# Modulation products in plain fp32 from the unsplit chunk on four column groups, and a latent projection in chunks of 352 columns

## The reference

```python
silu_c = jax.nn.silu(c); silu_cctx = jax.nn.silu(c_ctx)
for i in range(2):
    sh1, sc1, g1, sh2, sc2, g2 = jnp.split((silu_c @ mod_w[i] + mod_b[i])[:, None, :], 6, axis=-1)
    csh1, csc1, cg1, csh2, csc2, cg2 = jnp.split(silu_cctx @ mod_w[i] + mod_b[i], 6, axis=-1)
    a_lat = rms_norm(h_lat, norm_mix_g[i]) * (1 + sc1) + sh1      # a_ctx likewise, with csc1, csh1
    # i == 0: short convolution; i == 1: MLA attention, whose input projection is
    proj = h @ w_in            # 1024 x 1056: 768 query latents, 256 key/value latents, 32 rotary (pe)
    h_lat = h_lat + g1 * o_lat                                     # g2 after the FFN
```

## Time and profile before

| | us |
|---|---|
| median of 3 runs | 1528.9 |
| the profiled execution | 1531.93 |
| its span | 1530.1 |
| PE busy | 1435.3 |
| DVE busy | 923.9 |
| ACT busy | 651.2 |
| DMA, mean over the span | 141 GB/s |

### The profile page before, as it was taken

How to read it: one execution, slowest core, us unless ns; L and a number is a source line. 1 busy time by engine, 2 the same in 40 slices (tenths; PEclk the granted TensorE clock), 3 DMA queues, 4 the chain that set the end, 5 groups by cost and what they waited for, 6 DMA issues and landing times.

```text
span 1530.1 us, 18989 instructions
## 1 busy us (share of the span) xinstructions
PE 1435.3 (94%) x7536; PEld 1208.1 (79%) x7536; DVE 923.9 (60%) x1136; ACT 651.2 (43%) x743; POOL 0.2 (0%) x4
## 2 busy tenths in 40 slices
PE   6999889999989999999999999998989988899998
PEld 5877678888867887777888888886867766699997
DVE  5677676765666655766444453537566656646567
ACT  5364555544552222543132322225535554543442
POOL 0000000000000000000000000000000000000000
PEclk9999989999999999999999999999879998899999
DMA  8525565655642233233332414213221121344541
GB/s 307 196 94 219 196 234 217 229 208 222 245 154 83 83 143 118 75 118 127 148 120 99 163 56 164 96 69 121 93 76 46 69 96 61 120 166 171 203 175 56
DMA packets 18152, 215.58 MB, mean 141 GB/s; under 512 B 1960, under 2 KB 2984, under 8 KB 4784
## 3 DMA queue, kind: packets, MB, share of 16 engines
q1 hardware_dynamic: 16416, 209.67, 36.6%
q10 hardware_dynamic: 1680, 5.13, 0.9%
HBM read 213.74 MB, written 1.05 MB: 140 GB/s over the span
## 4 chain that ended last, share of the span: by engine, by line
PE 81%; DVE 10%; ACT 5%; issue 2%; ACTq 0%; DMA 0%; DVEq 0%
PE bank L401 24%; PE bank L403 23%; PE bank L402 23%; DVE w_lo L1430 6%; PE turned L418 3%; ACT w_hi L947 3%; PE small L831 2%; PE bank L825 2%; PE mod_ps L435 1%; PE mod_ps L436 1%; PE small L448 1%; PE small L458 1%; DVE x L1794 0%; DVE gated L1792 0%; DVE scaled L1471 0%
## 5 line engine op out<-in xcount | busy, mean ns | idle before, releaser
L1430 DVE TENSOR_TENSOR w_lo<-raw,w_hi 128x2048 fp32r<-128x2048 f32 (+1 forms) x214 | 460.3, 2193 | 82.5 <-ACT w_hi L947 82.1
L947 ACT ACTIVATE w_hi<-raw 128x2048 fp32r<-128x2048 f32 (+1 forms) x214 | 380.7, 1827 | 247.4 <-PE bank L403 179.9
L401 PE MATMUL bank<-act_hi,w_hi 128*128 128x256 f32 (+1 forms) x1208 | 400.1, 331 | 21.2 <-DVE w_lo L1430 12.8
L402 PE MATMUL bank<-act_lo,w_hi 128*128 128x256 f32 (+1 forms) x1208 | 396.7, 328 | 0.0
L403 PE MATMUL bank<-act_hi,w_lo 128*128 128x256 f32 (+1 forms) x1208 | 396.6, 328 | 0.0
L401 PEld LDWEIGHTS bank<-act_hi,w_hi 128*128 128x128 f32 x1208 | 232.4, 192 | 52.8 <-issue 17.8
L402 PEld LDWEIGHTS bank<-act_lo,w_hi 128*128 128x128 f32 x1208 | 232.5, 192 | 19.4
L403 PEld LDWEIGHTS bank<-act_hi,w_lo 128*128 128x128 f32 x1208 | 232.4, 192 | 19.2
L401 PE MATMUL bank<-w_hi,h_hi 128*128 128x512 f32 x392 | 157.3, 401 | 2.7 <-DVE h_lo L1848 1.5
L402 PE MATMUL bank<-w_lo,h_hi 128*128 128x512 f32 x392 | 155.9, 398 | 0.0
L403 PE MATMUL bank<-w_hi,h_lo 128*128 128x512 f32 x392 | 155.8, 397 | 0.0
(11 more groups left out here) (235 smaller groups left out, 1604.0 us busy)
## 6 DMA issues: line engine op xcount, KB each, us to landing
raw<-in_ffn SPq DMA_DIRECT2D x35, 2048.0 KB, 7.6
raw<-in_mlp SPq DMA_DIRECT2D x24, 2048.0 KB, 8.4
raw<-in_mod_gate SPq DMA_DIRECT2D x7, 2048.0 KB, 8.2
raw<-in_conv_in SPq DMA_DIRECT2D x8, 1536.0 KB, 6.5
raw<-in_w_gates SPq DMA_DIRECT2D x4, 2048.0 KB, 8.4
raw<-in_w_branch SPq DMA_DIRECT2D x4, 2048.0 KB, 8.6
raw<-in_mla_q SPq DMA_DIRECT2D x4, 1152.0 KB, 5.1
raw<-in_w_in SPq DMA_DIRECT2D x2, 2048.0 KB, 13.1
```

Source lines behind the costliest of these rows:

```text
L401: te.matmul(dst, sh, mh, start=(j == 0), stop=False)
L402: te.matmul(dst, sh, ml, start=False, stop=False)
L947: act.activation(w_hi[:, s, part], raw[:, s, part], ACT.Copy).then_inc(hi_ready, 1)
L1430: ve.tensor_tensor(w_lo[:, s, part], raw[:, s, part], w_hi[:, s, part].bitcast(f32), ALU.subtract).then_inc(lo_ready, 1)
```

## The change

1. `mod_product` reads the unsplit chunk in `raw` and multiplies it in plain fp32: eight matmuls (one per 128-row block) with a stationary operand of 32 columns and 512 moving columns. Block k writes partitions 32*(k%4) on of `mod_ps`, that is column group k%4 of the array; blocks k and k+4 share a group. ACT and DVE no longer split these 24 chunks, and they take no split slot; their raw slot is free when PE has read them (`mod_done`).
2. The condition window slides (`6 - 2j` to `38 - 2j`), so that two or four chunks of a batch land in different rows of each group and accumulate in one PSUM bank. There are 8 batches: ACT copies the whole bank to `mod_row` once per batch; for scales and shifts four transposes (`mod_turn`) and a DVE reduction over the four groups replace `mod_columns`; for gates `gate_rows` sums the groups with a 128-row selector. The gate bias is loaded by POOL into `gate` ahead of time and added by DVE.
3. The order is written out anew, with the loops of the MLP, the convolution and the first FFN unrolled: modulation products are one in front of each of the two branch products, one in MLP turns 0 and 1, one or two around the convolution and FFN norms, one after conv chunks 1 to 5, and three per FFN turn (12 in all there).
4. The MLA input is three chunks of 352 columns (2816 per partition), with the 32 rotary columns in the third; `w_pe` and its 96 matmuls are gone.

```diff
-            def mod_product():
-                s = chunk()
-                ...
-                    h, l = weights(s, k * COLS, (k + 1) * COLS)
-                    te.matmul(mod_ps[:, :], cond_w[:, k, :], h, start=(k == 0), stop=False)
-                    last = te.matmul(mod_ps[:, :], cond_w[:, k, :], l, start=False, stop=(k == KT - 1))
+            def mod_product(j, of):
+                ...
+                te.wait_ge(loaded[slot], 16 * (at + 1))
+                if j == 0 and n.n["batch"]:
+                    te.wait_ge(mod_row_ready, n.at("batch"))
+                ...
+                for k in range(KT):
+                    q = 32 * (k % 4)
+                    last = te.matmul(mod_ps[q:q + 32, :], cond[:, k, 6 - 2 * j:38 - 2 * j], raw[:, slot, k * COLS:(k + 1) * COLS],
+                                     start=(j == 0 and k < 4), stop=(j == of - 1 and k >= 4))
                 last.then_inc(mod_done, 1)
...
-            def mod_columns():
-                ...
+            def mod_turn():
+                te.wait_ge(mod_row_ready, n.at("batch"))
+                turn([mod_row[:, b * P:(b + 1) * P] for b in range(4)])
+            def gate_rows(batch, half, q):
+                te.wait_ge(sel_ready, 1)
+                te.wait_ge(mod_row_ready, batch)
                 small_bank()
+                te.matmul(small[:, :], sel[:, 2 * half + q, :], mod_row[:, :], start=True, stop=True).then_inc(small_done, 1)
...
+            def mlp_turn(i):
+                up(i == 0)
                 up()
                 te.wait_ge(hidden_ready, n.at("hidden", 2))
                 down()
+                if i < 2:
+                    mod_product(2 + i, 4)
...
+            for f in range(1, KT):
+                if f == 1:
+                    mod_product(1, 2)
+                elif f < 6:
+                    mod_product(f - 2, 4)
                 conv_in()
+                if f < 5:
+                    gate_rows(2, (f - 1) // 2, (f - 1) % 2)
...
+            for i in range(4):
+                mod_product((3 * i) % 4 if i < 3 else 1, 4 if i < 3 else 2)
                 gate_up()
+                if i == 1:
+                    mod_turn()
+                mod_product((3 * i + 1) % 4 if i < 3 else 0, 4 if i < 3 else 2)
                 gate_up()
+                if i == 2:
+                    mod_turn()
+                mod_product((3 * i + 2) % 4 if i < 2 else 0 if i == 2 else 1, 4 if i < 2 else 2)
                 down0_all()
...
+            for c in range(3):
+                s = chunk()
+                for tt in range(2 * NT if c == 2 else NT):
+                    b = unit()
+                    if tt == NT:
+                        te.wait_ge(norm_ready, n.step("norm", 4))
+                    first = 0 if tt < NT else MLA_W - KVL - ROPE
+                    product(b[:, first:MLA_W], [(act_rows(tt, k), weights(s, k * MLA_W + first, (k + 1) * MLA_W)) for k in range(KT)],
+                            second=4 if tt == 0 else None).then_inc(gemm_done, 1)
```

More of the change, by code:

```diff
@@ L319, in _, with slot_free, load_mla_in @@
         def _(sp):
[L320 to L328, removed]
+            def slot_free(at):
+                if at < 2:
+                    return
+                if STREAM[at - 2][3]:
+                    sp.wait_ge(mod_done, MOD_AT.index(at - 2) + 1)
+                else:
+                    sp.wait_ge(lo_ready, 2 * (WEIGHT_AT.index(at - 2) + 1))
+            def load_mla_in(i, slot):
+                first, second = (a["mla_in"][c].rearrange("p (k n) -> p k n", k=KT) for c in range(2))
+                dst = raw[:, slot, 0:KT * MLA_W].rearrange("p (k n) -> p k n", k=KT)
+                if i == 0:
+                    sp.dma_start(dst, first[:, :, 0:MLA_W]).then_inc(loaded[slot], 16)
+                elif i == 1:
+                    cut = COLS - MLA_W
+                    sp.dma_start(dst[:, :, 0:cut], first[:, :, MLA_W:COLS]).then_inc(loaded[slot], 16)
+                    sp.dma_start(dst[:, :, cut:MLA_W], second[:, :, 0:MLA_W - cut]).then_inc(rest_loaded[0], 16)
+                else:
+                    cut = MLA_W - ROPE
+                    sp.dma_start(dst[:, :, 0:cut], second[:, :, COLS - cut:COLS]).then_inc(loaded[slot], 16)
+                    sp.dma_start(dst[:, :, cut:MLA_W], a["w_pe"]).then_inc(rest_loaded[1], 16)
             for t in range(NT):
@@ L335, in _ @@
             sp.dma_start(rows[:, :], a["rows"].rearrange("(o n) -> o n", o=1).to_broadcast([P, NROW])).then_inc(const_loaded, 16)
[L336 to L354, removed]
+            for i, (section, k, width, _) in enumerate(STREAM):
+                slot_free(i)
+                if section == "mla_in":
+                    load_mla_in(k, i % 2)
+                else:
+                    sp.dma_start(raw[:, i % 2, 0:width], a[section][k]).then_inc(loaded[i % 2], 16)
             for t in range(NT):
@@ L923, in _ @@
             down1(1, 2, 0)
-            assert n.n["chunk"] == STREAM, (n.n["chunk"], STREAM)
+            assert n.n["chunk"] == WEIGHTS and n.n["mod"] == len(MOD_AT) and n.n["batch"] == 8
         @block.scalar
@@ L1076, in _ @@
             split()
-            mod_copy()
-            split()
             n.step("unit", 4)
-            n.step("small")
             for half in range(2):
@@ L1156, in mlp_turn @@
                     high(1, 0)
-                split()
+                split(CHUNK if i < 3 else 3072)
                 n.step("unit", 2)
-                if first:
+                if i == 1:
+                    mod_turned()
+                if i == 2:
                     high(1, 1)
-            mlp_turn(first=True)
-            with n.loop(act, 3, split=6, unit=8, square=4, mod=2, small=2):
-                mlp_turn()
+            for i in range(4):
+                mlp_turn(i)
             def mlp_rows(t):
@@ L1376, in _ @@
                     plain_hi(act_dst(act_hi, 0, half, t))
-            mod_copy(7)
-            for cb in range(2):
-                split()
-                n.step("unit", 2)
-            n.step("small")
+            n.step("unit", 2)
+            split()
+            n.step("unit", 2)
             for t in range(NT):
@@ L1855, in down_gated @@
                         add_gated(tt, cb, tt // NT, False)
-            hidden_chunk(0)
+            hidden_chunk(0, 2048, True)
             down_gated()
-            with n.loop(ve, 4, split=4, unit=16, small=1, mod_small=1, silu=4, hidden=4, chain=8) as i:
-                hidden_chunk(0, early=True)
+            for i in range(4):
+                hidden_chunk(0)
+                if i == 1:
+                    mod_read(2)
                 hidden_chunk(2)
-                mod_read(12, i, 1)
+                if i == 2:
+                    mod_read(3)
                 down_gated()
@@ L1865, in _ @@
             hidden_chunk(2)
-            split()
+            split(KT * MLA_W)
             def down_rows0(tt):
```

534 lines of the change are left out of this document (236 added, 298 removed).

## The result

The changed kernel takes 1446.26 us (median of 4 runs, 1443.83 to 1446.94); the kernel before took 1529.61 us on the same chip (1528.64 to 1532.94). The ratio is 0.9446, 95% interval 0.9431 to 0.9461. I forecast 1492 and a range of 1432 to 1550. So the kernel became faster, as expected, but by 83 us instead of 37. The time is that of the rival *four at once* (1444), which I had given a chance of 0.22.

What follows compares the result with a forecast made beforehand. PE was taken to bound the kernel (busy 94% of the span), so only its stream or waits save time. Stage terms summed to -131.0 + 23m, -36.7 us with m = 4.1: 1492 us, range 1432 to 1550.

Steps and rivals of the forecast that it cites:

- four at once: Rival for the modulation product: four column groups stream at once, m = 2.0 us, -85 us, 1444; chance 0.22.
- m = 4.1: Chosen cost in us of one modulation product after the change: records start in program order, nine steps; chance 0.48.
- The ledger: Stage-by-stage sum of forecast changes against PE's profile windows; -36.7 us in all with m = 4.1.
- the FFN stage: First FFN: four products, four columns and idle time go, 12 products and two turns come; -20.5 + 12m = +28.7 us.
- -131 + 23m: Forecast change of the whole kernel in us, m the cost per product; 24 products, one of them hidden.
- The latent input and what is behind it: MLA input in three chunks without the narrow matmuls, -21.7 us; 1.5 more behind it; -23.2 us together.
- Before the last projection: Window where a product covered the end of `act_lo`; of 4.7 us 1.8 stays, -2.9 us.
- The branches: Stage from 118.30 to 155.57 with two branch and two modulation products; 2m - 9.4, forecast -1.2 us.
- No overlap: Rival, decided in FFN and convolution: column groups don't overlap, m = 7.1 us, +32 us, 1561; chance 0.16.
- the turning point: Product cost at which the whole change is even: m = 5.7 us, above which no overlap decides.
- The clock: Rival: 32-column products lower the granted clock, 2.6 us each, 60 us over 23, about 1552; chance 0.04.
- A late transfer: Rival, above all around the FFN norm: up to 10 us on the forecast, 1502; 0.10 shared with a mix.

## Why the prediction was wrong

**The step that failed** is the choice of the product's price: "I take m = 4.1: the trace shows an in-order stream wherever I looked, and two records per fp32 matmul." The 0.43 us per record beside it was right, and about 0.1 us for each change was a little low (0.33 us for both, not 0.2); the working by which sixteen records take nine steps was wrong. It rests on "the second overlaps only the first record of the next matmul". Measured are four steps and not nine, 1.86 us from start to start and 2.05 us in PE's stream, and the run with the same group twice in a row shows that a record doesn't wait for an earlier one of another group. In the trace of before no two neighbouring matmuls stand on separate column groups, so its stream would look in order under either rule. That was no evidence for order; I read it as some. Each of the three values had a mechanism, and no row told them apart; I gave the middle one 0.48 and the right one 0.22.

**The rule that I drew on** did not hold here: that matmuls start strictly in program order (the Trainium skill, "TensorE: Matmul & The Clock Gate", Part 3, What overlaps and what doesn't). The same page's gain for tiles (3.07 times for four row tiles) was nearer; measured are 3.75 times for four column groups, from start to start.

**The ledger held.** With m = 2.05 its terms give -83.9, and the spans differ by -85.4. No stage is off by over 5 us; the FFN stage, where half of the products stand, is off by 2.0. Its slope holds too. With the same 0.19 us on top of the start-to-start time, m is 7.17 for one group and 3.75 for two. By -131 + 23m the first should be 33.9 us slower than before and the second 44.8 faster; measured are 2.1% slower, 32 us, and 3.2% faster, 49 us.

**Terms that were off by size:**
- The latent input and what is behind it: -18.8 instead of -23.2. The input itself gave 19.6 of 21.7. Behind it I counted another 1.5 for a product that goes, but it had stood under the norm of the queries, and 0.8 us more are needed there, at a granted clock of 0.74.
- Before the last projection: nothing instead of -2.9. The wait went as I said, but the product had also kept PE busy; after, the projection starts at a clock of 0.50. With the waits filled the clock is 1.00 and this stage 3.5 us shorter (40.59 instead of 44.04), which fits that reason.
- The branches (1.3 us short): the last `act_lo` still ends late, with waits of 2.2 and 1.4 us, and the clock is 0.50 from 148.3 to 155.1.
- Not counted at all: the rest until the latent input (-4.4), where a shorter split stands ahead of the norm's rows. The wait for these rows is 1.5 us instead of 3.3, and the granted clock of the stage 1.00 instead of 0.95.

**The rivals.** *Four at once* was right, by 2 us (m = 2.0, measured 2.05). *No overlap* and the turning point were right in size, but the chip overlaps. *The clock*: the 32-column fp32 products don't lower it (1.00 in the FFN with twelve of them in 289.41 us). It did fall behind waits that nothing covers any more, and in narrow matmuls (32 moving columns) without a wait. *A late transfer* doesn't show: PE waits for no `raw`.

## What to carry to other kernels

Small products whose moving operand is wide can run on four column groups at once, in plain fp32: sixteen records of 512 columns in 1.86 us, and the order in which they are issued costs next to nothing. What such a product costs is read from the matmul ahead of it to the second one behind it, since the steps at both of its ends are longer too. A stream that looks in order is no evidence of what happens when its parts are independent: if no row can tell the rivals apart, the chances should say so. And when work under a wait is made cheaper or taken out, look at the granted clock behind the wait: either put other due work there, or fill it.

## What the runs showed of the hardware

- Records of plain fp32 matmuls to different column groups run side by side and past each other: 6.98, 3.56 and 1.86 us for one, two and four groups; 1.87 us with the same group twice in a row.
- The granted clock was 0.50 behind a stretch of 15.50 us (175.20 to 190.70) in which PE was busy for 3.98 us. It was 1.00 there when PE was busy for 12.52 us of it. Matmuls whose result is dropped held it there.
- In the 96 matmuls with 32 moving columns PE was busy all the time and the granted clock was 0.63: 1.00 at first (0.11 us each), then 0.50 (0.21 us each). The FFN's products, with 32 stationary and 512 moving columns, left it at 1.00.
- A product of four rounds of 0.43 us makes PE's stream 2.05 us longer, 0.33 more than its rounds: 0.09 ahead of it, 0.14 within and 0.10 in the step behind. The 0.10 also stands behind a wait between matmuls of full width (793.28 to 793.61 in before).
